# Filler products on TensorE between the stages of a two-block model

## The chip, the cores and the metric

The kernel runs on one core of a Trainium2 chip. The metric is the device time of one execution in microseconds (us), the median of the runs.

## The reference, cut to what matters

Two transformer blocks run one after the other on 512 tokens of width 1024, in float32. Every sublayer begins with an RMS norm and ends by adding to the residual `x`.

```python
h = rms_norm(x, g) @ w_in                      # first block: sparse attention with compressed keys, and latent attention
x = x + concat(o_nsa, o_mla) @ w_out
x = x + (silu(n(x) @ w_gate) * (n(x) @ w_up)) @ w_down
x = x + short_conv(n(x) @ od_w_in) @ od_w_out
x = x + moe_top2(n(x))                         # 8 experts, each token takes the two highest
# second block: a gated linear recurrence, attention with decay, and a chunked recurrence (RWKV) side by side
x = x + concat(lru, fox, rwkv) @ w_out
x = x + group_experts(n(x))                    # 4 groups of 4 experts
```

## The kernel before

The program is a row of some 27 stages. A stage (`stage`, L36) is a block with one instruction list for each engine; its engines meet each other by semaphores, and at its end all of them drain and meet at a barrier. So a stage ends when its last engine does, and the next begins a little over a microsecond later.

Large products are made by `split_product` (L552): each operand is a rounded high part and a low part in fp32r, and three products (L555, L556, L557) of 128 rows, 128 columns and 512 moving columns are accumulated. The high parts are made by ScalarE (ACT), the low parts by VectorE (DVE), so TensorE (PE) waits at the start of every such stage until the first weights and activations are split. Products of plain float32 operands, such as L391, L993 or L3478, stand in the trace as two records each, a transpose (L67, L122, L195) as one.

The stages that the change touches, in order of time, with the time at which TensorE first does real work in each: `split_features` for "ev_in" (plain products to 46, split products from 49.6); `norms_and_hidden`, the stage "ev_hidden" (to 147), whose end is set by DVE (L2158); `compressed_scores` (from 159.8), with transposes L2209, then a softmax on DVE and ACT, then transposes L2215 at 183.9; three `attention` stages, ending at 303, 416 and 1886, the last with a `beside` object that adds products of the recurrence; `add_projection` three times (419.9, 1010.9, 2013.4); `norm_transpose` three times (L122, ending at 477, 863 and 1626); `gated_parts` (484.5); `split_features` for "od_in" (870.4 to 1006); `norm_route` twice, which transposes the normed rows (L195, one tile of 128 tokens after another as DVE makes them) and multiplies them with a router of 8 or 20 columns (L204), 1066.7 to 1084 and 2071.7 to 2092; `plan_passes` twice (L993 to L1007), where DVE computes each token's place from counts that TensorE makes; `sorted_passes` twice (first split products at 1113 and 2117.7), which run the experts' weights past the gathered tokens; `second_inputs` (1628.9 to 1792); the chunked recurrence `rwkv` with its stage "rw_chunks" (L3478 and others, 1886.6 to 1994); and its last stage "rw_end" (L3582, L3585), where DVE ends with L3630.

`keep_awake` (L64) is there already: 24 transposes of the unit matrix at the start of each norm. It writes bank 7 of PSUM.

## Time and profile before

| what | value |
|---|---|
| median of 3 runs | 2325.05 us (2324.07 to 2329.28) |
| profiled execution, its time | 2320.53 us |
| its span | 2319.0 us |
| mean granted TensorE clock | 0.935 |
| TensorE matmul busy | 2068.7 us, 89% |
| VectorE, ScalarE, GpSimd busy | 1285.5, 994.2 and 185.8 us |

### The profile page before, as it was taken

How to read it: one execution, taken by the hardware profiler on the slowest of the kernel's cores; microseconds unless marked ns; L12 is line 12 of the kernel's file. 1: busy time of each engine (PE TensorE's matmuls, PEld its weight loads, DVE VectorE, ACT ScalarE, POOL GpSimd, SP SyncE). 2: the span in 40 equal slices, each digit the busy share in tenths (PEclk: the TensorE clock that was granted, in tenths of full speed). 3: DMA queues.
4: the chain of work that ended last, by engine and by line, in shares of the span. 5: the costliest groups of instructions: out<-in, count | busy, mean ns of one | idle time of the engine just before them, and what ended most of it. 6: DMA issues, size and time to landing. Idle time of an engine off the chain costs nothing. (4 is left out here: it accounts for less than half of the span.)

```text
span 2319.0 us, 31287 instructions
## 1 busy us (share of the span) xinstructions
PE 2068.7 (89%) x11611; PEld 1570.0 (68%) x11611; DVE 1285.5 (55%) x1814; ACT 994.2 (43%) x1308; POOL 185.8 (8%) x182
## 2 busy tenths in 40 slices
PE   7966898889999989997899999997898789686998
PEld 5743334668888877876777888786476359575776
DVE  3367746353133234444566666888367745525888
ACT  2135736342223222221566665774243643404774
POOL 0010000000000000000311010111112200002111
PEclk9978988989999999997899999999999789886999
DMA  8006101144144125002778777995320000126996
GB/s 249 6 14 237 47 10 45 37 127 123 43 122 127 37 83 194 1 37 83 256 269 282 278 270 281 370 391 216 88 73 28 12 1 1 74 84 174 399 373 258
DMA packets 220713, 336.29 MB, mean 145 GB/s; under 512 B 50413, under 2 KB 135309, under 8 KB 220606
## 3 DMA queue, kind: packets, MB, share of 16 engines
q1 hardware_dynamic: 213470, 314.53, 40.0%
q0 software_dynamic: 7136, 20.34, 2.3%
q8 instruction: 66, 1.08, 0.2%
q14 instruction: 41, 0.34, 0.0%
HBM read 306.82 MB, written 26.95 MB: 144 GB/s over the span
## 5 line engine op out<-in xcount | busy, mean ns | idle before, releaser
L1526 DVE TENSOR_TENSOR moe_pass_wL<-moe_pass_w,moe_pass_wH 128x2048 fp32r<-128x2048 f32 (+1 forms) x144 | 303.4, 2112 | 115.8 <-ACT moe_pass_wH L1450 111.3
L1450 ACT ACTIVATE moe_pass_wH<-moe_pass_w 128x2048 fp32r<-128x2048 f32 (+1 forms) x144 | 254.7, 1772 | 129.6 <-PE PS L557 97.2
L555 PE MATMUL PS<-moe_pass_wL,moe_pass_xgH 128*128 128x512 f32 (+1 forms) x384 | 148.3, 386 | 9.1 <-DVE moe_pass_xgL L1531 4.8
L1526 DVE TENSOR_TENSOR hm_pass_wL<-hm_pass_w,hm_pass_wH 128x2048 fp32r<-128x2048 f32 x60 | 135.9, 2288 | 34.8 <-ACT hm_pass_wH L1450 34.7
L555 PE MATMUL PS<-xnT_low,ffn_upH 128*128 128x512 f32 x352 | 140.3, 399 | 7.4 <-DVE xnT_low L873 7.1
L557 PE MATMUL PS<-moe_pass_wH,moe_pass_xgH 128*128 128x512 f32 (+1 forms) x384 | 143.5, 374 | 0.0
L556 PE MATMUL PS<-moe_pass_wH,moe_pass_xgL 128*128 128x512 f32 (+1 forms) x384 | 143.5, 374 | 0.0
L557 PE MATMUL PS<-ffn_xH,ffn_upH 128*128 128x512 f32 x352 | 139.9, 397 | 0.0
L556 PE MATMUL PS<-ffn_xH,ffn_up_low 128*128 128x512 f32 x352 | 138.4, 393 | 0.0
L1450 ACT ACTIVATE hm_pass_wH<-hm_pass_w 128x2048 fp32r<-128x2048 f32 x60 | 112.2, 1910 | 17.1 <-PEq L1340 6.0
L880 DVE TENSOR_TENSOR ffn_hT<-ffn_sg,PS 128x512 f32<-128x512 f32 x22 | 15.1, 688 | 167.7 <-PE PS L557 167.7
L839 ACT ACTIVATE ffn_sg<-PS 128x512 f32<-128x512 f32 x22 | 13.2, 599 | 187.8 <-PE PS L557 187.8
L555 PEld LDWEIGHTS PS<-moe_pass_wL,moe_pass_xgH 128*128 128x128 f32 x384 | 72.5, 189 | 28.5 <-issue 11.8
L555 PE MATMUL PS<-xnT_low,od_in_wH 128*128 128x512 f32 x192 | 77.3, 403 | 7.1 <-DVE od_W_low L689 7.1
L555 PEld LDWEIGHTS PS<-xnT_low,ffn_upH 128*128 128x128 f32 x352 | 66.6, 189 | 22.4 <-DVE ffn_up_low L858 7.3
L557 PEld LDWEIGHTS PS<-moe_pass_wH,moe_pass_xgH 128*128 128x128 f32 x384 | 72.6, 189 | 10.6
L556 PEld LDWEIGHTS PS<-moe_pass_wH,moe_pass_xgL 128*128 128x128 f32 x384 | 72.7, 189 | 9.4
L557 PEld LDWEIGHTS PS<-ffn_xH,ffn_upH 128*128 128x128 f32 x352 | 66.9, 190 | 15.9
L556 PEld LDWEIGHTS PS<-ffn_xH,ffn_up_low 128*128 128x128 f32 x352 | 66.7, 190 | 15.8
L556 PE MATMUL PS<-od_xH,od_W_low 128*128 128x512 f32 x192 | 76.7, 399 | 0.0
L555 PE MATMUL PS<-hm_pass_wL,hm_pass_xgH 128*128 128x512 f32 x160 | 65.3, 408 | 12.7 <-DVE hm_pass_wL L1526 7.1
L557 PE MATMUL PS<-od_xH,od_in_wH 128*128 128x512 f32 x192 | 75.7, 394 | 0.0
(841 smaller groups left out, 4868.6 us busy)
## 6 DMA issues: line engine op xcount, KB each, us to landing
moe_pass_w<-in_moe_w_down SPq DMA_DIRECT2D x40, 1024.0 KB, 4.9
moe_pass_w<-in_moe_w_gate SPq DMA_DIRECT2D x32, 1024.0 KB, 5.2
moe_pass_w<-in_moe_w_up SPq DMA_DIRECT2D x32, 1024.0 KB, 7.2
hm_pass_w<-in_exp_w_gate SPq DMA_DIRECT2D x40, 512.0 KB, 7.7
hm_pass_w<-in_exp_w_up SPq DMA_DIRECT2D x40, 512.0 KB, 6.9
hm_pass_w<-in_exp_w_down SPq DMA_DIRECT2D x40, 512.0 KB
od_W<-in_od_w_in SPq DMA_DIRECT2D x12, 1024.0 KB, 8.2
moe_pass_w<-in_moe_w_gate SPq DMA_DIRECT2D x16, 768.0 KB
```

Source lines behind the costliest of these rows:

```text
L555: nc.tensor.matmul(out, lh, rl, start=start, stop=False)
L556: nc.tensor.matmul(out, ll, rh, start=False, stop=False)
L557: return nc.tensor.matmul(out, lh, rh, start=False, stop=stop)
L839: nc.scalar.activation(sg[:, c % 2], PS[:, c % 2, :], ACT.Silu).then_inc(s["silu"], 1)
L880: nc.vector.tensor_tensor(hT[:, c], sg[:, c % 2], PS[:, 2 + c % 2, :], ALU.mult).then_inc(s["hidden"], 1)
L1450: nc.scalar.activation(wH[:, i % S, 0:n], w[:, i % R, 0:n], ACT.Copy).then_inc(s["high"], 1)
L1526: nc.vector.tensor_tensor(wL[:, i % S, 0:n], w[:, i % R, 0:n], f32(wH[:, i % S, 0:n]), ALU.subtract) \
```

## The change

A helper `stay_busy` issues `n` products of the unit matrix with a matrix of ones, float32, 128 by 128 by 128, into a PSUM bank that nothing reads any more or yet. Nothing reads their result. There are 18 calls of it, which come up 33 times, since helpers run more than once, with 463 products in all, in the order of TensorE's own instructions; before some of the calls stand waits, so that the bank is free. `norm_transpose` has a new semaphore `placed`, which counts its DVE copies out of PSUM. All other engines' instructions are as before.

```diff
+def stay_busy(nc, C, n, bank=7):
+    for _ in range(n):
+        nc.tensor.matmul(C.PS[:, bank, 0:P], C.ident[:, :], C.ones[:, :], start=True, stop=True)
...
 def norm_transpose(...):
...
-                                            PS[:, 2 * t + h].rearrange("p (k c) -> p k c", k=4), g, ALU.mult)
+                                            PS[:, 2 * t + h].rearrange("p (k c) -> p k c", k=4), g, ALU.mult).then_inc(s["placed"], 1)
...
                 ins.then_inc(s["turned"], 1)
+            pe.wait_ge(s["placed"], 1)
+            stay_busy(nc, C, 12, 0)
...
 def norm_route(...):
             keep_awake(nc, C)
+            stay_busy(nc, C, 16)
             turn(0)
...
 def attention(...):
                 beside.tensor_end(pe, s)
+            pe.wait_ge(s["exped"], U)
+            stay_busy(nc, C, 16 if beside else 5, 0)
...
 def add_projection(...):
         def _(pe):
+            stay_busy(nc, C, 12)
             for k in range(KD):
...
 def split_features(...):
+            if NP:
+                pe.wait_ge(s["taken"], 8)
+            stay_busy(nc, C, 12)
             for j, (w, wL, take, ready) in enumerate(jobs):
...
+            pe.wait_ge(s["taken"], NP + len(jobs) - 2)
+            stay_busy(nc, C, 6, (NP + len(jobs) - 3) % 8)
...
 def gated_parts(...):
             pe.sem_inc(s["down_free"], DR)
+            stay_busy(nc, C, 12)
...
-def plan_passes(nc, C, name, tiles, hits, token_rows, kept, pick, weigh, exps, weights=None, token_weights=None, ring=None):
+def plan_passes(nc, C, name, tiles, hits, token_rows, kept, pick, weigh, exps, busy, weights=None, token_weights=None, ring=None):
+            stay_busy(nc, C, busy[0])
             pe.wait_ge(s["masked"], 1)
...
             ins.then_inc(s["placed"], 1)
+            stay_busy(nc, C, busy[1])
             pe.wait_ge(s["hot"], 1)
...
             ins.then_inc(s["found"], 1)
+            stay_busy(nc, C, busy[2])
             if weights is not None:
...
 def sorted_passes(...):
+            stay_busy(nc, C, 8)
             n = passes(pe)
             gather(0, OVER > 0)
+            stay_busy(nc, C, 14)
...
             one_pass(n, False, True)
+            stay_busy(nc, C, 8, 3)
             pe.wait_ge(s["spots"], 1)
...
 def norms_and_hidden(...):
                 hidden(n)
+            pe.wait_ge(s["gelu"], 1)
+            stay_busy(nc, C, 40, 4)
...
 def compressed_scores(...):
                 ins.then_inc(s["by_token"], 1)
+            stay_busy(nc, C, 36, 0)
             pe.wait_ge(s["values_taken"], 2)
             pe.wait_ge(s["weighed"], 1)
...
 # plan_passes: busy is (10, 20, 16) for moe_plan and (5, 4, 20) for hm_plan
 def second_inputs(...):
             ins.then_inc(s["made"], 1)
+            stay_busy(nc, C, 12)
             for j in range(NJ):
...
+            pe.wait_ge(s["normed"], 8)
+            stay_busy(nc, C, 18)
...
 # rwkv, stage rw_end, after L3585
+                stay_busy(nc, C, 44)
```

## Rows read from the trace of the kernel before

**Rows 1.** Span and mean granted clock of the core.

```profile
core 0: 2319.0 us, clock 0.935
```

**Rows 2.** Timeline: start us, us, engine line operation, tiles, shapes, records, [idle before].

```profile
1088.06 0.64 PE L993 MATMUL PS<-moe_plan_mask,ones 128*128 128x32 f32 x2 [4.02 <-DVE moe_plan_mask L1019]
...
1095.48 0.80 PE L1001 MATMUL PS<-moe_plan_token,moe_plan_hot 128*128 128x1 f32 x3 [5.12 <-DVE moe_plan_hot L1071]
```

**Rows 3.** Window of L3478: us, PE busy (records), PEld busy, clock, DMA share, GB/s.

```profile
1909.66:1910.55 0.89, 0.89 (x8) 0.86 (x8) 1.00 0.00 0
```

**Rows 4.** Windows: us, busy (count) of PE, PEld, DVE, ACT, POOL, clock, DMA, GB/s.

```profile
469.10:472.51 3.41, 3.41 (x18) 3.41 (x17) 2.35 (x6) 2.59 (x6) 0.00 (x0) 0.50 0.66 191
472.51:475.92 3.41, 3.41 (x29) 3.13 (x28) 1.58 (x3) 3.41 (x4) 0.00 (x0) 1.00 1.16 290
```

**Rows 5.** Windows: first split products of six stages; columns as in rows 4.

```profile
49.55:52.67 3.12, 3.12 (x7) 2.48 (x8) 3.12 (x6) 0.00 (x0) 0.00 (x0) 0.50 1.12 371
419.93:424.73 4.80, 4.80 (x11) 3.76 (x12) 4.80 (x6) 4.80 (x8) 0.00 (x0) 0.50 0.79 300
484.47:489.58 5.11, 5.11 (x12) 4.05 (x13) 5.11 (x8) 4.17 (x5) 0.00 (x0) 0.50 0.37 119
870.43:875.29 4.86, 4.86 (x12) 3.79 (x13) 4.69 (x7) 2.76 (x5) 0.00 (x0) 0.50 1.07 354
1010.91:1015.23 4.32, 4.32 (x10) 3.48 (x11) 4.32 (x6) 4.32 (x7) 0.00 (x0) 0.50 0.85 337
2013.37:2018.75 5.38, 5.38 (x13) 4.23 (x14) 5.38 (x7) 5.38 (x9) 0.00 (x0) 0.50 0.00 0
sum 27.59, PE 27.59 PEld 21.78 DVE 27.42 ACT 21.43 POOL 0.00; mean PE 4.60 PEld 3.63 DVE 4.57 ACT 3.57 POOL 0.00
```

**Rows 6.** Windows: other stretches at low clock, and dense split products at 560.

```profile
159.84:165.31 5.47, 5.46 (x10) 2.89 (x11) 1.83 (x4) 0.00 (x0) 0.07 (x1) 0.50 0.00 1
183.88:185.79 1.91, 1.91 (x8) 1.54 (x8) 0.00 (x0) 0.00 (x0) 0.00 (x0) 0.50 0.00 0
335.98:359.87 23.89, 23.40 (x27) 7.83 (x25) 15.37 (x22) 2.35 (x5) 0.00 (x0) 0.50 0.19 44
1066.74:1084.03 17.29, 17.29 (x96) 17.20 (x96) 4.92 (x5) 3.37 (x6) 0.00 (x0) 0.60 0.30 121
1112.99:1117.63 4.64, 4.64 (x11) 3.68 (x12) 2.29 (x1) 1.24 (x1) 3.80 (x3) 0.50 0.99 238
1629.63:1633.05 3.42, 3.42 (x5) 1.35 (x4) 0.00 (x0) 3.42 (x7) 3.36 (x3) 0.50 0.42 138
1796.89:1800.30 3.41, 3.41 (x9) 0.94 (x8) 0.50 (x4) 1.02 (x3) 0.00 (x0) 0.50 0.61 195
1886.64:1902.70 16.06, 16.06 (x90) 11.72 (x91) 8.47 (x13) 4.23 (x13) 0.00 (x0) 0.50 0.01 2
2071.74:2092.10 20.36, 20.35 (x96) 20.23 (x96) 4.91 (x5) 3.37 (x6) 0.00 (x0) 0.50 0.48 168
560.00:640.00 80.00, 79.70 (x348) 64.89 (x347) 21.33 (x29) 17.73 (x27) 0.00 (x0) 1.00 0.18 56
```

**Rows 7.** Timeline: ends and starts of stages around six places.

```profile
149.13 0.57 ACT L2106 ACTIVATE ev_hid<-PS 128x64 f32<-128x64 f32 x4
...
157.89 0.63 DVE L2158 COPY ev_hid<-ev_hid 128x128 f32<-128x128 f32 x4
...
302.59 0.69 DVE L523 COPY ev_yT<-PS 128x512 f32<-128x512 f32 x1 [4.15 <-PE PS L419]
...
416.95 0.63 ACT L596 ACTIVATE ev_out_yH<-ev_yT 128x512 fp32r<-128x512 f32 x1 [6.26 <-PEq L42]
...
419.93 0.76 PE L555 MATMUL PS<-ev_front_low,ev_out_yH 128*128 128x512 f32 x1 [4.51 <-DVE ev_front_low L619]
...
1997.29 1.98 PE L3585 MATMUL PS<-rw_end_sq,ones 128*128 128x512 f32 x4 [0.59 <-ACT rw_end_sq L3593]
...
2008.24 1.28 DVE L3630 TENSOR_TENSOR s_yT<-rw_Bt,rw_gl 128x512 f32<-128x512 f32 x2
```

More of the change, by code:

```diff
@@ L67, in keep_awake @@
         nc.tensor.transpose(C.PS[:, 7, 0:P], C.ident[:, :], C.ident[:, :])
+def stay_busy(nc, C, n, bank=7):
+    for _ in range(n):
+        nc.tensor.matmul(C.PS[:, bank, 0:P], C.ident[:, :], C.ones[:, :], start=True, stop=True)
 def norm_transpose(nc, C, x, gain, xnT, xs, name, loads=None, gain_loaded=None, clear=None, ahead=None):
-    with ExitStack() as mem, stage(nc, name, "squared_a squared_v mean root rstd scaled turned") as (block, s):
+    with ExitStack() as mem, stage(nc, name, "squared_a squared_v mean root rstd scaled turned placed") as (block, s):
         ss = mem.enter_context(nc.sbuf_tensor(name + "_ss", [P, 4, NT], F32))
@@ L2615, in moe_top2 @@
             norm_route(nc, C, "moe_norm", x, xs, xnT, gx[:, :], wr, br[:, :], score, NE, loads, (loaded, 48), C.token_rows["moe_pass"], kept, constants)
-            Q = plan_passes(nc, C, "moe_plan", tiles, [one, two], C.token_rows["moe_pass"], kept, pick, weigh, exps, ring=ring)
+            Q = plan_passes(nc, C, "moe_plan", tiles, [one, two], C.token_rows["moe_pass"], kept, pick, weigh, exps, (10, 20, 16), ring=ring)
         w1, w2 = pair[:, 0], pair[:, 2]
@@ L2692, in moe_groups @@
             norm_route(nc, C, "hm_norm", x, xs, xnT, gx[:, :], wr, br[:, :], score, NG + NE, loads, (loaded, 80), C.token_rows["hm_pass"], kept, constants)
-            Q = plan_passes(nc, C, "hm_plan", tiles, [group], C.token_rows["hm_pass"], kept, pick, weigh, exps, w[:, :, :], C.token_weights)
+            Q = plan_passes(nc, C, "hm_plan", tiles, [group], C.token_rows["hm_pass"], kept, pick, weigh, exps, (5, 4, 20), w[:, :, :], C.token_weights)
         sorted_passes(nc, C, "hm_pass", x, xnT, ring, tiles, Q, NG, PG * F, PG, 0, 0, NG, None, store_tile)
```

## The prediction

> **What bounds the kernel now.** I read the span with its clock first: TensorE is granted 0.935 of its clock on average [rows 1], so (1 - 0.935) x 2 x 2319 = about 301 us pass at the low of its two levels, 1.2 GHz. That sets the most that any cure could give: were TensorE the last to be ready in all of them, 151 us. The other two questions are where these stretches lie, and in which of them TensorE is the one that is awaited; for those I went through windows and timeline.
>
> They lie in three kinds of place. First, six stages that begin with split products: PE waits some microseconds for the first splits and starts at 0.50, busy throughout, 27.59 us together [rows 5]. Second, the beginnings of stages with float32 products or transposes, and the two routers [rows 6]. Third, stretches where PE is busy without a break and yet at 0.50: 335.98 to 359.87, where most products use 8 of the 128 rows, and most of the two routers, whose products stream only 8 or 20 columns [rows 6]. The third kind says that a busy PE is not enough to hold the clock; the shape of the work counts. A filler has 128 rows, 128 loaded columns and 128 streamed ones, like the transposes of `keep_awake`, and a stretch of those began at 0.50 and was at 1.00 afterwards, with nothing but transposes on PE [rows 4]. So I expect a filler to count as work.
>
> **What one filler costs.** One call of a float32 product is two records [rows 2] (L993 is one call). At the high level eight records of 128 columns took 0.89 us [rows 3], 0.112 each, so a filler is 0.224 us. At the low level the hm router's 96 records took 20.36 us [rows 6], 0.212 each, and a filler 0.42. Groups of 12, 16, 36, 40 and 44 take 2.7, 3.6, 8.1, 9.0 and 9.9 us at the high level, 5.1, 6.8, 15.3, 17.0 and 18.7 at the low. All 463 are 104 or 196 us.
>
> **What covers them.** PE waits at these places anyway. In ev_out the stage's first ACT instruction is at 416.95 and the first product at 419.93 [rows 7]: 3.0 us for 12 fillers of 2.7. The four other stages that open with 12 just before split products, and ev_in behind its plain products, are built in the same way (ACT rounds, DVE subtracts, then PE). In rw_end PE is done at 1999.3 and DVE at 2009.5 [rows 7]: 10.2 us for 44 of 9.9. Before L1001 PE idles 5.12 us [rows 2]: 20 of 4.5. Where the cover fits, an edit costs nothing so long as the clock is high when the group begins; at the low level the same group is late by the whole difference.
>
> **What it takes away, step by step.**
>
> 1. First products of six stages. 65 records in 27.59 us at 0.50 [rows 5], against 80 us / 348 = 0.230 each in dense stretches [rows 6]: 27.6 - 65 x 0.230 = -12.6 us. DVE's low parts come at one per 0.64 us (8 in 5.11, the third row) and a k-step of three products takes 0.69, so PE stays the last.
> 2. Four short float32 stretches [rows 6]. The first products of the compressed scores, 5.47 us, behind 40 fillers; the last transposes there, 1.91, behind 36; the first products of second_inputs, 3.42, behind 12 of the norm; the first of the decayed attention, 3.41, behind 18. All dense, so half: -7.1 us.
> 3. The chunk stage, 1886.64 to 1902.70, 16.06 us with PE busy throughout. The 16 fillers at the end of the attention stage leave a gap of about 1 us. Half would be 8.0, but DVE is busy 8.47 us of these [rows 6] and becomes the bound in its first third: -6.0.
> 4. The routers. hm: 20.36 us at 0.50 for 96 records [rows 6]. All at the high level they would take 96 x 0.112 = 10.8, or -9.5; but its L204 products are those that let the clock fall even while PE is busy, so I keep the last third at the low level: -6.8. moe: 17.29 us at mean 0.60 [rows 6], whose middle was already at 1.00: -2.0.
> 5. Plans and passes. The counts and the one-hot products of moe_plan, and the first 4.64 us of products of its passes [rows 6], would win 2.8 + 2.1; but the plan is entered at the low level that the router leaves, and its first 10 fillers then take 4.2 us against 4.02 idle, of which only some 2.8 lie in the stage [rows 2]: +1.3. Net -3.6. In hm's I count -0.5: its passes' first products are followed by waits for weights anyway.
>
> **What it adds.** Fillers that stand at the end of a stage and are not covered. The 40 of ev_hidden wait for L2106, which ends at 149.7; DVE ends the stage at 158.5 [rows 7]. The engine had idled before, so the clock falls by then in most executions, and I let a third of the 40 run low: 149.7 + 9.0 + 2.4 = 161.1, or +2.4 (bounds: +0.2 all high, +8.2 all low). The 5 behind the first attention take 1.1 us while DVE's last copy, 0.69 us, ends the stage [rows 7]: +0.4, and again in the latent one. The other endings (6 fillers of ev_in and od_in, 12 of s_norm, 18 of second_inputs, 16 of the decayed attention) overshoot by +0.5, +0.3, +0.9, +0.5 and +0.2 by the same reckoning, which are estimates from the same kinds of rows, and the start of ev_in by +0.2. Sum: +5.8 us. The new `placed` increments ride on instructions that are there; their wait was met long before by the first copy.
>
> **The sum.** -12.6 - 7.1 - 6.0 - 8.8 - 3.6 - 0.5 + 5.8 = -32.8 us against the profiled execution's 2320.5, or 2287.7. Its own time lies 4.5 us under the median of the runs, so the same difference from the median is 2292.3. Every term supposes that the clock was high when a group began, and where in a group it changes is chance, so some of 33 places will not come off; I take off a tenth of the gain and forecast 2295 us.
>
> The Trainium skill bears on this in "TensorE: Matmul & The Clock Gate", Part 1. It says that the gate opens with activity and closes after idleness, and that for a model the ramp penalty is below 1% of a typical kernel span. By that, less than 23 us are to be had and the time is above 2302. This trace shows 27.59 us at the low level in the first kind of place alone [rows 5], and 301 in all, because every stage boundary may bring a new ramp. The trace outweighs it, and the sum above doesn't use it.
>
> **The rivals.**
>
> *Half of it* (2303 to 2315, about 2309). The idle stretches that matter are broken by a barrier of over a microsecond, in which no filler can run, and the fillers in front of and behind it may be too short in some places. Against it: with the groups in place little more than that barrier is left of the idle 4.51 us before ev_out's first product [rows 7]. If only the first kind and the short stretches come off and the costs stay, -12.6 - 7.1 + 5.8 = -13.9 us: 2311. The skill's below 1% would end in or just above this case. Chance 0.17.
>
> *The fillers run at the low level* (slower). Mechanism: each group begins after idleness, at 0.50, and the unit matrix, mostly zeros, doesn't raise it. Price: 44 fillers in rw_end take 18.7 against 10.2 of cover, the 40 in ev_hidden 17.0 against 8.8, 12 in ev_out 5.1 against 3.0: of 19.4 us that these 96 gain in length 18.8 are exposed. For all 463 that makes about 90 us and no gain: 2415. Mixed, with share p of the fillers low, gain and loss meet at 33(1 - p) = 90p, p = 0.27: from a quarter of the groups upwards the change loses. For it: most groups do begin after a wait, and the routers were at 0.50 while busy. Against it: the transposes of the same matrix raised the clock [rows 4]. Chance 0.06, and mostly near the point of balance, 2330 to 2345.
>
> *It shifts the waits only* (within 0.2%, 2320 to 2330). PE's first products come sooner, and the next wait, for weights or DVE, takes the gain back. For it: DVE is busy for nearly the whole of the six starts [rows 5]. Against it: later in such stages PE is without gaps (79.70 of 80 us from 560 on [rows 6]), so a start that is earlier by 2 us ends the stage earlier by 2 us. Chance 0.07.
>
> *All of it and more* (2275 to 2283). ev_hidden's 40 all high, hm router wholly high, moe_plan not late: -2.2 - 2.7 - 1.3 more, and no tenth lost. Chance 0.05.
>
> The forecast's own case, 2283 to 2303, has 0.65.
>
> **Range and chances.** From 2281 to 2313 it holds the main case, most of the half case and some of the last: 0.8. Faster by over 0.2% (4.65 us, about what a measurement can tell from no change) is main, half and more: 0.87. Same 0.07, slower 0.06.
>
> **What would show it right or wrong.** The mean clock should rise from 0.935 to about 0.965. The six starts should be at 1.00 with records 0.23 us apart; one at 0.50 refutes step 1 for that stage. The chunk stage should last about 6 us less until the first common record after 1902.7. In the routers the first transposes should be at 1.00, and part of L204 still at 0.50. Fillers should be 0.224 us apart; groups at 0.42 are the slow rival. After the last filler of ev_hidden and of both attentions no other engine should be the last of its stage. Wrong would be the sum, rather than the mechanism, if the clock is up and the span isn't down.

## The result and the profile after

The changed kernel takes 2293.74 us, the median of 4 executions (2289.0 to 2299.9), beside 2324.56 for the kernel before (4, 2321.4 to 2329.3). The ratio is 0.9877, with a 95% interval of 0.9849 to 0.9906: faster by 1.2%. The forecast was 2295.0, with 2281 to 2313 around it.

The first row to read is that of the core, against [rows 1]:

```profile
core 0: 2291.6 us, clock 0.970
```

The span fell by 27.4 us. Time at the low level fell from about 301 us to (1 - 0.970) x 2 x 2291.6 = about 137, so 164 us less. Two records at the high level take as long as one at the low, so work that TensorE alone holds up would have given half of that, 82 us; the span gave 27. In most of the stretches TensorE was not the engine that was waited for, or fillers were what ran in them.

The windows that begin at each of the six first split products, cut behind the same number of records as in [rows 5] (the counts in brackets are those of all records that touch the window):

```profile
48.17:49.90 1.73, 1.73 (x7) 1.42 (x8) 1.73 (x4) 0.00 (x0) 0.00 (x0) 1.00 1.05 372
411.45:414.06 2.61, 2.60 (x12) 2.15 (x12) 2.61 (x4) 2.61 (x5) 0.00 (x0) 1.00 1.01 405
473.83:476.68 2.85, 2.85 (x13) 2.33 (x13) 2.85 (x6) 2.85 (x4) 0.00 (x0) 1.00 0.65 212
857.31:860.18 2.87, 2.87 (x12) 2.36 (x13) 2.87 (x5) 2.78 (x5) 0.00 (x0) 1.00 1.08 365
995.91:998.32 2.41, 2.40 (x10) 1.96 (x11) 2.41 (x4) 2.41 (x5) 0.00 (x0) 1.00 1.02 420
1985.43:1988.54 3.11, 3.11 (x14) 2.52 (x15) 3.11 (x4) 3.11 (x6) 0.00 (x0) 1.00 0.00 0
sum 15.58, PE 15.57 PEld 12.75 DVE 15.58 ACT 13.76 POOL 0.00; mean PE 2.59 PEld 2.12 DVE 2.60 ACT 2.29 POOL 0.00
```

All six stand at 1.00 and PE is still busy throughout: nothing new is waited for, the same work is simply done at nearly twice the rate. The kernel before over the same records, in the same way up to the start of the next one, has this sum, and in its chunk stage, over the first 90 records, this row:

```profile
sum 28.16, PE 28.16 PEld 22.16 DVE 27.75 ACT 21.66 POOL 0.00; mean PE 4.69 PEld 3.69 DVE 4.62 ACT 3.61 POOL 0.00
...
1886.64:1902.81 16.17, 16.17 (x90) 11.83 (x92) 8.47 (x13) 4.34 (x13) 0.00 (x0) 0.50 0.01 2
```

Windows of the changed kernel: the chunk stage, the hm router's fillers, the router itself, and the last stretch of hm_plan:

```profile
1863.18:1873.02 9.84, 9.43 (x91) 6.96 (x93) 8.13 (x13) 4.29 (x13) 0.00 (x0) 1.00 0.00 1
2035.13:2038.90 3.77, 3.74 (x34) 3.55 (x32) 0.27 (x2) 0.21 (x1) 0.00 (x0) 1.00 0.45 56
2041.40:2061.55 20.15, 19.84 (x96) 19.51 (x96) 5.16 (x6) 3.37 (x6) 0.00 (x0) 0.52 0.47 165
2070.26:2076.30 6.04, 6.04 (x29) 6.04 (x30) 4.36 (x28) 0.42 (x2) 1.08 (x1) 0.50 0.30 88
```

The first 90 records of the chunk stage went from 16.17 us at 0.50 to 9.84 at 1.00, and the mark of a new bound is there: PE is no longer busy throughout (9.43), and DVE is busy for 8.13. The 16 fillers ahead of the hm router ran at 1.00; PE then idled 2.5 us for DVE, and the router ran its 96 records in 20.15 us, as slowly as in [rows 6]. hm_plan's last 20 fillers then ran at 0.50 for their first 6 us too, ahead of the product that spreads the weights.

Stage lengths, from the time at which the last engine ends one stage to that at which it ends the next, POOL's gathers counted (us, good to some 0.3). "Again" is a second profile of the changed kernel, below; it differs from "after" by chance alone. Stages that moved by less than 0.3 us are left out.

| stage | before | after | again |
|---|---|---|---|
| ev_in | 91.7 | 89.3 | 89.3 |
| ev_hidden | 45.5 | 46.4 | 50.7 |
| ev_compressed | 28.6 | 25.0 | 25.0 |
| first attention | 116.2 | 115.1 | 116.1 |
| latent heads | 56.7 | 53.7 | 57.1 |
| latent attention | 56.2 | 56.7 | 55.3 |
| ev_out | 51.2 | 49.0 | 49.0 |
| ffn | 372.8 | 370.4 | 370.5 |
| od_in | 140.9 | 139.0 | 140.4 |
| od_out | 51.6 | 49.7 | 49.7 |
| moe_norm | 25.6 | 23.3 | 25.3 |
| moe_plan | 19.3 | 20.0 | 19.0 |
| moe_pass | 512.2 | 509.6 | 509.7 |
| s_norm | 12.3 | 13.5 | 13.3 |
| s_in | 167.1 | 166.0 | 166.0 |
| s_fox | 90.4 | 87.9 | 89.1 |
| chunk stage | 108.3 | 103.9 | 105.3 |
| s_out | 52.1 | 49.6 | 49.6 |
| hm_norm | 30.8 | 30.3 | 21.8 |
| hm_plan | 15.9 | 17.3 | 17.1 |
| hm_pass | 207.8 | 209.9 | 209.1 |

The losses that repeat are those of hm_plan, hm_pass, s_norm and ev_hidden. In moe_plan it depends on which engine ends the stage. Before, that is POOL, with the second of two gathers:

```profile
1102.63 0.89 POOL L987 DMA_INDIRECT moe_plan_xto<-moe_pass_tokens,moe_plan_idxo  x1 [0.30 <-issue]
```

Its timeline after, on PE and POOL:

```profile
1066.11 4.03 PE L73 MATMUL PS<-ones,ident 128*128 128x128 f32 x20 [1.31 <-PEq L42]
1069.97 0.31 PE L1012 MATMUL PS<-moe_plan_mask,ones 128*128 128x32 f32 x2
...
1079.53 5.47 PE L73 MATMUL PS<-ones,ident 128*128 128x128 f32 x32
...
1082.23 0.88 POOL L1005 DMA_INDIRECT moe_plan_xto<-moe_pass_tokens,moe_plan_idxo  x1 [0.30 <-issue]
```

The last 16 fillers (32 records, L73) run from 1079.53 to 1085.00, the first 3.4 us of it at the low level, while POOL's last gather ends at 1083.11. TensorE, with filling only, ends the stage, 1.9 us late. POOL alone would have ended it 18.1 us after the stage before it, where it took 19.3 in the kernel before: the earlier groups had gained 1.2 us, and the last one spent 1.9. (The expectations below count moe_plan and moe_pass as 17.1 and 514.3 us in the kernel before; that leaves POOL's gathers out, which hold the stage open. The loss of 2.8 us in moe_plan and a part of the gain of 4.7 in moe_pass come from there.)

### The profile page after: what moved, and what is told of

It reads as the page before. It is cut to its first block and busy times, and to the rows that moved or that the text cites. A ratio compares the mean times of both kernels' runs of the same rounds, so it can differ in the third digit from the quotient of the medians.

```text
span 2291.6 us, 33139 instructions
## 1 busy us (share of the span) xinstructions
PE 2137.0 (93%) x12537; PEld 1652.5 (72%) x12537; DVE 1284.4 (56%) x1814; ACT 994.1 (43%) x1308; POOL 186.9 (8%) x182
## 5 line engine op out<-in xcount | busy, mean ns | idle before, releaser
L73 PE MATMUL PS<-ones,ident 128*128 128x128 f32 x926 | 120.9, 293 | 13.4 <-PEq L42 11.1
L73 PEld LDWEIGHTS PS<-ones,ident 128*128 128x128 f32 x926 | 116.9, 207 | 18.3 <-issue 15.4
L857 ACT ACTIVATE ffn_sg<-PS 128x512 f32<-128x512 f32 x22 | 13.2, 598 | 185.0 <-PE PS L568 185.0
L566 PE MATMUL PS<-hm_pass_wL,hm_pass_xgH 128*128 128x512 f32 x160 | 64.9, 405 | 12.6 <-DVE hm_pass_wL L1550 10.4
```

What stands on the lines that cost most here:

```text
L73: nc.tensor.matmul(C.PS[:, bank, 0:P], C.ident[:, :], C.ones[:, :], start=True, stop=True)
L566: nc.tensor.matmul(out, lh, rl, start=start, stop=False)
L857: nc.scalar.activation(sg[:, c % 2], PS[:, c % 2, :], ACT.Silu).then_inc(s["silu"], 1)
```

## The experiments

Each run is compared with executions of the kernel before on its own chip; medians of the kernel before in these comparisons lie between 2322.0 and 2324.6 us.

| run | median us | ratio, 95% | clock |
|---|---|---|---|
| narrow | 2359.9 | 1.0156 (1.0130 to 1.0182) | 0.931 |
| rows32 | 2359.1 | 1.0154 (1.0131 to 1.0177) | 0.931 |
| recur | 2316.7 | 0.9976 (0.9963 to 0.9988) | 0.940 |
| padonly | 2310.6 | 0.9947 (0.9928 to 0.9966) | 0.940 |
| nostarts | 2304.0 | 0.9918 (0.9899 to 0.9937) | 0.961 |
| starts | 2301.0 | 0.9905 (0.9880 to 0.9930) | 0.943 |
| again | 2294.8 | 0.9874 (0.9850 to 0.9897) | 0.969 |
| pad | 2291.1 | 0.9852 (0.9834 to 0.9871) | 0.971 |
| noplans | 2289.3 | 0.9856 (0.9829 to 0.9883) | 0.963 |
| planend | 2286.8 | 0.9842 (0.9827 to 0.9857) | 0.971 |
| router | 2286.2 | 0.9840 (0.9814 to 0.9866) | 0.975 |
| best | 2279.7 | 0.9830 (0.9806 to 0.9853) | 0.978 |

**Fillers of 8 columns.** All 463 fillers at their places, each with next to nothing to stream; the 128 by 128 unit matrix is still loaded for each.

```diff
-        nc.tensor.matmul(C.PS[:, bank, 0:P], C.ident[:, :], C.ones[:, :], start=True, stop=True)
+        nc.tensor.matmul(C.PS[:, bank, 0:8], C.ident[:, :], C.ones[:, 0:8], start=True, stop=True)
```

> Every filler keeps its place and its count but multiplies only 8 columns of the ones, not 128, so TensorE is given as many instructions at the same times and very little work in them. My theory, that the gain is the clock, which stays high when fillers give TensorE real work where it would idle: the granted clock goes back to that of before (0.935, against 0.970), the six split-product starts are at 0.50 again, and the time is that of before within some 6 us, 2318 to 2331 us. Rival: it is enough that TensorE is not idle, whatever it does: then the clock is 0.970 and the time about 2290 to 2294, the fillers being shorter. Rival: the gain comes from the waits and the order that the edits bring: 2294 too, but with the clock of before.

**Fillers of 32 rows.**

```diff
-        nc.tensor.matmul(C.PS[:, bank, 0:P], C.ident[:, :], C.ones[:, :], start=True, stop=True)
+        nc.tensor.matmul(C.PS[:, bank, 0:P], C.ident[0:32, :], C.ones[0:32, :], start=True, stop=True)
```

> Every filler keeps place, count and its 128 columns, but contracts over 32 rows of the unit matrix and of the ones in place of 128. It should last as long (0.27 us at the high rate). If the clock asks only whether TensorE streams columns, time and clock are those of the changed kernel, 2294 us and 0.970. If the rows in use count too, as the 12 spreading products over 8 rows suggest, behind which the clock fell while TensorE was busy without a gap, the fillers are worth a quarter: clock near 0.94 and 2320 to 2345 us, between the narrow fillers (2359.9) and the kernel before.

Both came out alike, 35 us *slower* than the kernel before. The groups of the filler line, minimum, median and maximum of a record in ns, in the changed kernel, then in the narrow one, then with 32 rows:

```profile
L73 PE MATMUL PS<-ones,ident x926: 270/275/582, 44.9 to 2281.5; 128*128 128x128 f32 x186
```

```profile
L73 PE MATMUL PS<-ones,ident x926: 170/361/381, 44.9 to 2347.1; 128*128 128x8 f32 x186
```

```profile
L73 PE MATMUL PS<-ones,ident x926: 270/416/577, 44.9 to 2355.9; 32*128 32x128 f32 x186
```

The minimum is that of the high level, the median shows where most of them ran: 275 of 270 in the changed kernel, but 361 and 416 in these two, more than half of them at the low level. (One record follows another after 0.112 us at the high level [rows 3], so records of 270 ns overlap.) By the clock's own stretches in the three traces, 99 of the 926 filler records begin at the low level in the changed kernel, 519 in the narrow one and 497 with 32 rows. The six starts took 25.55 us in the narrow kernel and 26.73 with 32 rows, against 28.16 before and 15.58 with real fillers:

```profile
sum 25.55, PE 25.55 PEld 20.16 DVE 24.88 ACT 18.02 POOL 0.00; mean PE 4.26 PEld 3.36 DVE 4.15 ACT 3.00 POOL 0.00
```

```profile
sum 26.73, PE 26.73 PEld 21.04 DVE 25.92 ACT 17.60 POOL 0.00; mean PE 4.45 PEld 3.51 DVE 4.32 ACT 2.93 POOL 0.00
```

So the order of the work, the added waits and TensorE being given instructions bring nothing. What pays is that a filler uses the array: its streamed columns and its rows both count, 8 columns are too few and so are 32 rows; nothing between these and 128 was tried. Both rivals of the narrow run fell (that it is enough not to be idle, and that the waits and the order bring the gain), and so did my size for the two: I had the narrow one back at the time of before and the one of 32 rows between, and had forgotten that a filler that does not raise the clock is itself a long one. ev_hidden went from 45.5 to 53.3 and 53.6 us, moe_plan from 19.3 to 27.4 and 28.3, the last recurrence step from 15.7 to 19.7 and 19.9. These two runs show what the prediction's slow rival costs.

**Fillers at the six starts only, and all but those.** The first keeps the groups of 12 in `norm_transpose`, `add_projection`, `split_features` and `gated_parts` and takes all others out; the second takes just these out.

```diff
-            stay_busy(nc, C, 12)        # add_projection, split_features, gated_parts
-            stay_busy(nc, C, 12, 0)     # norm_transpose
```

> Only the fillers at the split-product starts are kept (12 at the end of norm_transpose, 12 at the start of add_projection, 12 in split_features behind the pair products, 12 in gated_parts); all others are taken out. In the changed kernel the six starts together are 13.2 us shorter than in the kernel before and s_norm is 1.2 longer. If each place pays for itself alone, this version is about 12 to 14 us below the kernel before, 2310 to 2313 us, and the other fillers hold the remaining 18. Rival: places depend on one another (an earlier stage's fillers decide whether the clock is high when the next one begins): then this one is either within 5 us of the changed kernel or less than 8 below the kernel before.

> The changed kernel without the fillers at the split-product starts, the complement of the run that had only those (2301.0 us, 23.6 below the kernel before, where its own six stages were 11 to 13 us shorter in its profile). If what that run gained is these fillers' own, taking them away from the changed kernel costs as much, about 2316 us. If each place is worth only what the profiles show, 13 us, it is about 2307 us, and the remainder of that run's gain was the scatter between executions (2299.1 to 2307.8).

In the first the six windows sum to 15.93 us, five at 1.00 and one at 0.88, in the second to 25.27, five of those six at clocks of 0.51 to 0.63 and one at 0.50. The windows' rows of the two sums:

```profile
sum 15.93, PE 15.93 PEld 13.01 DVE 15.93 ACT 14.06 POOL 0.00; mean PE 2.65 PEld 2.17 DVE 2.65 ACT 2.34 POOL 0.00
```

```profile
sum 25.27, PE 25.26 PEld 19.94 DVE 25.27 ACT 20.12 POOL 0.00; mean PE 4.21 PEld 3.32 DVE 4.21 ACT 3.35 POOL 0.00
```

The starts are high because of the groups just ahead of them, and low without them. In profiled executions the two spans are 13.0 and 16.0 us under the kernel before, together 29.0, where the whole change has 27.4: the parts add up. In medians they don't: the starts alone gained 23.6 us, more than the 12 to 14 forecast and than either rival, yet taking them away cost only 10 (2304.0, where 2307 or 2316 was expected). The profiled execution of the starts alone was 6.8 us above its own median and that of the kernel before some 5 below its own. The starts are worth between 10 and 24 us by the times, 12.6 by the windows; I trust the windows.

**The recurrence alone.** 12 fillers within s_in and 18 at its end, just ahead of s_fox, and 44 in the last recurrence step, all others taken out. (The expectation puts the first two into s_fox; they stand in `second_inputs`. The 16 at the end of s_fox, which the prediction's step 3 rests on, are not in this run.)

> Only the fillers of the recurrence: 12 and 18 in s_fox and 44 in the last recurrence step; nothing else is added to the kernel before. In the changed kernel s_fox is 2.4 us shorter and the chunk stage 4.4, the last step unchanged. If these come from their own fillers the time is about 7 us below the kernel before, 2317 to 2319 us (my prediction had 6.0 less 0.2 for this part). Rival: s_fox gains from the fillers ahead of it (end of s_in), then 4 to 5 us. Rival: the chunk stage's gain comes from the stage before it: none, 2324.

The time is 6.4 us below (12 executions), and in its profile s_fox took 87.8 us and the chunk stage 103.7, as in the changed kernel (87.9 and 103.9). For s_fox the fillers just ahead of it explain that: in this run its start is at the high level, and in the profiles without them it isn't. For the chunk stage they do not. No filler runs between 1793.4 and 1990.2, and the stage still began at 0.50, but only for 6.5 us, where the kernel before had 17.2. So this run does not show where the chunk stage's gain comes from. What does is the set of profiles: the eight with the 16 real fillers ahead all began the stage at 1.00 and took 101.6 to 105.3 us; without them it was 108.3, 108.3 and 107.4, and 103.7 here, and with the fillers of 8 columns and of 32 rows 108.4 and 109.4.

**Without the fillers of plans and passes.** `stay_busy` taken out of `plan_passes` and `sorted_passes`.

> The changed kernel without the fillers of plan_passes and sorted_passes. Stage by stage from before to after, moe_plan grew by 2.8 us, moe_pass fell by 4.7, hm_plan grew by 1.4 and hm_pass by 2.0: together +1.5. If these differences are the fillers' own doing, taking them out gives 1.5 us back, about 2292 us, with moe_plan near 17.1, moe_pass near 514, hm_plan near 15.9 and hm_pass near 208. Rival: the pass differences come from where the clock happens to be high at the start of a pass and not from the fillers: then the plans fall by 4 us and the passes stay, about 2289 to 2290. Rival: fillers of the plan do hold the clock for the first pass: 2297 or more.

2289.3 us (2285.0 to 2298.3), so no slower than the changed kernel, whose 8 executions here have a median of 2294.1 (2288.6 to 2299.9). That is less than the scatter can settle, but it has *less* clock (0.963 against 0.970). By stages: moe_plan 19.2 (from 20.0 and 19.0 in the two profiles of the changed kernel), hm_plan 15.8 (from 17.3 and 17.1), moe_pass 510.9 (from 509.6 and 509.7). The pass loses 1.3 us without its groups, and the plans lose some 1 to 2 with theirs. hm_pass is 211.8, and it is 211.8 in the run of the recurrence alone too, so the 2.0 us that it had grown by are not the fillers'; the changed kernel itself also came out at 209.1.

**Fillers within the routers.**

```diff
             keep_awake(nc, C)
-            stay_busy(nc, C, 16)
+            stay_busy(nc, C, 16 if n < 16 else 28)
             turn(0)
             for t in range(1, NT):
                 turn(t)
                 logits(t - 1)
+                stay_busy(nc, C, 3)
```

> Three fillers behind each of the first three groups of logits in norm_route, in both routers, and 28 fillers instead of 16 ahead of the first turn in the second router, where TensorE idled 2.53 us behind the fillers and the clock then stayed at 0.50 through the whole router. If the low clock there comes from the little work that logits of 8 or 20 columns give TensorE, together with that idle stretch, hm_norm falls by 5 to 7 us and hm_plan by 1 to 2 (its fillers run at the high rate), moe_norm and moe_plan by 0 to 3: 2284 to 2288 us in all. Rival: the router is paced by the placing copies of ScalarE and VectorE or by loads: the added 18 fillers, at 0.22 to 0.42 us for one, lengthen it by 2 to 5 us: 2296 to 2299.

2286.2 us, within the 2284 to 2288 forecast, hm_norm 23.8 us, at 1.00 in the router. That seems to bear the expectation out. But noplans, without this edit, had 22.7, and even the run with starts only had 24.0; that is what the next run was for.

**The changed kernel again.**

> The changed kernel, word for word, for a second profile and more executions. In its first profile hm_norm took 30.3 us with TensorE at 0.50 throughout the router, but the run without fillers in the plans, with the same router, had 22.7, and the run with fillers at the starts only, with none in the router, had 24.0. If the phase of the clock is chance from one execution to the next, hm_norm can come out anywhere from 22 to 31 us here, the stages that are always at the high level repeat within 0.1 us, and the median is 2291 to 2296. If instead 30.3 us belongs to this kernel's timing, it comes out at 30 to 31 us again.

hm_norm took 21.8 us. The router's window in this profile, to be held against the third of the four rows above (20.15 us at 0.52):

```profile
2053.11:2064.82 11.71, 11.37 (x96) 10.91 (x96) 5.16 (x6) 3.36 (x6) 0.00 (x0) 1.00 0.82 286
```

The same 96 records, the same code: 11.7 us or 20.2. What differed is the wait ahead of the first transpose, here and in the first profile:

```profile
2053.11 2.35 PE L203 MATMUL PS<-ident,hm_xs 128*128 128x128 f32 x16 [0.75 <-DVE hm_xs L187]
```

```profile
2041.40 3.17 PE L203 MATMUL PS<-ident,hm_xs 128*128 128x128 f32 x16 [2.53 <-DVE hm_xs L187]
```

Here the transposes of `keep_awake` ran at the low level, took 4.48 us in place of 2.81, and so covered most of the wait. In the other profiles with 16 fillers the transposes also ran high behind a wait of 1.13 us (noplans) and with hardly any (nostarts), and low behind one of 2.25 (pad); in nostarts and noplans the clock fell later, within the router. And ev_hidden, whose 40 fillers were the largest cost in the prediction, came out at 50.7 here, 46.4 in the first profile. So a single profile cannot say what a group of fillers is worth in such a stage. Of the five profiles taken with 16 fillers ahead of this router, with or without the plan's, hm_norm had 30.3, 21.8, 22.7, 25.7 and 27.1 us. The three with the edit above had 23.8, 23.8 and 23.8. The edit costs 2 us against the best case, and in these three profiles no bad one came up.

**Router fillers, without the last group of each plan.**

```diff
-... exps, (10, 20, 16), ring=ring)
+... exps, (10, 20, 0), ring=ring)
-... exps, (5, 4, 20), w[:, :, :], C.token_weights)
+... exps, (5, 4, 0), w[:, :, :], C.token_weights)
```

> The kernel of the run with fillers in the routers, less the last group of fillers in each plan (16 behind the last products of moe_plan, 20 in hm_plan ahead of the product that spreads the weights). In the changed kernel those groups ran at the low rate, held the stage open behind POOL's gathers (moe_plan) and delayed the spreading product (hm_plan). Theory: they only cost, so moe_plan falls from 19.0 to about 16.5 us and hm_plan from 17.3 to about 15.9, the passes stay where they are, and the time is about 2282 us (2286.2 with them). Rival: they hold the clock for the start of the pass, which loses 3 to 4 us without them: 2286 again.

No gain: 2286.8 against 2286.2 us. moe_plan stayed where it was (19.3 us, from 19.0), since POOL ends it:

```profile
1085.66 0.88 POOL L1006 DMA_INDIRECT moe_plan_xto<-moe_pass_tokens,moe_plan_idxo  x1 [0.30 <-issue]
```

In the router run its last fillers had ended only 0.3 us behind these gathers, so there was next to nothing to win. hm_plan hardly moved (17.3 to 17.1), so its last 20 fillers are not what it had lost by; the first 5 are. They run at the low level and hold up the counts that DVE waits for, as these two lines of the kernel before and of the changed one show, 2.3 and 3.4 us behind the end of the stage before:

```profile
2094.71 0.61 PE L993 MATMUL PS<-hm_plan_mask,ones 128*128 128x16 f32 x2 [2.62 <-DVE hm_plan_mask L1021]
```

```profile
2064.86 0.45 PE L1012 MATMUL PS<-hm_plan_mask,ones 128*128 128x16 f32 x2
```

moe_pass went from 510.2 to 509.3 and od_in happened to be 1.3 longer. So the time is the rival's, but not for its reason: the passes lost nothing, and the theory failed in that the groups cost next to nothing where they stood.

**Padding the products of 8 rows.** The clock of the changed kernel falls at 332.1 us in the latent heads, where PE has no gap. The cure there is not a filler but rows: the same products with zeros below the 8 rows in use.

```diff
-        pick, spread = sb("pick", [P, 6, NH]), sb("spread", [NH, 6, P])
+        pick, spread = sb("pick", [P, 6, NH]), sb("spread", [P, 6, P])
...
+                             (spread[NH:P].rearrange("p a n -> p (a n)"), zero[NH:P, 0:6 * P])):
...
-        rs, tt, ec = sb("rs", [NH, 2, SEQ]), sb("tt", [NH, 2, SEQ]), sb("ec", [P, 1])
+        rs, tt, ec = sb("rs", [P, 2, SEQ]), sb("tt", [NH, 2, SEQ]), sb("ec", [P, 1])
...
+            step(nc.gpsimd.memset(rs[:, :, :], 0.0))
```

> The changed kernel, with the 12 spreading products of the latent heads contracted over 128 rows instead of 8: the two operands are padded with zeros below the 8 rows in use, which costs one memset on POOL and one small transfer, and no time on TensorE (a product of 512 columns takes 0.50 us at the high rate with either). In the changed kernel the clock falls to 0.50 at 332.1 us, with TensorE busy without a gap since 324.7 on products of 8 rows, and stays there for 17 us. If the few rows are what lets it fall, it stays at 1.00 here even though the added rows hold zeros, and the stage falls from 53.7 to 46 to 49 us, the time to 2287 to 2290 us (VectorE is busy 7.5 of 7.9 us there and takes part of the gain). Rival: zeros draw nothing and the clock falls as before: 2294. Rival: VectorE paces the stage whatever the clock: clock 1.00, stage above 52 us, 2293.

> The kernel before, without any filler, with the spreading products of the latent heads padded with zeros from 8 to 128 rows. With the fillers this made the stage 5.1 us shorter (53.7 to 48.6) and the next 2.0 longer. If the rows alone keep the clock, it holds without fillers too: the stage falls from 56.7 to 49 to 51 us and the time to 2317 to 2320 us (2323 before). Rival: without fillers the clock is low at the stage's start and the gain is under 2 us.

Timeline of PE in the changed kernel:

```profile
327.47 6.06 PE L2365 MATMUL PS<-lh_rs,ev_spread 8*128 8x512 f32 x12
333.46 2.07 PE L2362 MATMUL PS<-ev_ukv,ev_latent 128*128 128x512 f32 x2
335.46 10.61 PE L2365 MATMUL PS<-lh_rs,ev_spread 8*128 8x512 f32 x12
346.00 4.41 PE L2362 MATMUL PS<-ev_ukv,ev_latent 128*128 128x512 f32 x6
```

and of the padded one:

```profile
329.46 5.42 PE L2367 MATMUL PS<-lh_rs,ev_spread 128*128 128x512 f32 x12
334.71 1.02 PE L2364 MATMUL PS<-ev_ukv,ev_latent 128*128 128x512 f32 x2
335.57 5.31 PE L2367 MATMUL PS<-lh_rs,ev_spread 128*128 128x512 f32 x12
340.72 2.74 PE L2364 MATMUL PS<-ev_ukv,ev_latent 128*128 128x512 f32 x6
...
348.74 5.04 PE L400 MATMUL PS<-ev_km,xnT 96*128 96x128 f32 x10 [5.28 <-PEq L42]
```

The windows of the two, before and behind the place where the clock fell in the changed kernel:

```profile
324.71:332.11 7.40, 7.40 (x18) 2.50 (x17) 3.85 (x6) 2.59 (x3) 0.00 (x0) 1.00 0.09 22
332.11:349.18 17.07, 17.07 (x20) 5.83 (x19) 13.47 (x19) 1.20 (x2) 0.00 (x0) 0.50 0.22 52
```

```profile
329.46:343.50 14.04, 14.00 (x33) 5.99 (x32) 12.27 (x18) 4.38 (x7) 0.00 (x0) 1.00 0.20 47
347.63:354.46 6.83, 5.72 (x13) 3.82 (x14) 3.59 (x13) 2.39 (x9) 0.00 (x0) 0.50 0.70 245
```

In the changed kernel PE is busy for 17.07 of 17.07 us and stands at 0.50. Padded, the second group of 12 records takes 5.31 us where it took 10.61, and the stage 48.6 where it took 53.7. The rows that were added hold zeros, and they count all the same. In the eleven profiles without padding this stage took 53.7 to 57.1 us, in the three with it 48.5, 48.5 and 48.6. The last two rows of the padded kernel (L400 in its timeline, 347.63 in its windows) show a part of the gain given back: PE now idles 5.28 us, mostly because the transfers and DVE's products into `ev_km` are still on their way (to 347.5 and 347.9), and the attention starts at the low level (58.6 us against 56.7). The median is 3 us under the changed kernel's, too little to tell from its scatter; the stage shows the gain.

In the kernel without fillers padding made the stage 48.5 us, from 56.7, and the next 54.9, from 56.2; the ratio is 0.9947. I had expected a median 3 to 6 us lower, and it is 11.4 lower. The two stages' 8.2 and 1.3 us are seen in the profile; the remaining 2 us are within the interval (8 to 17 us) and need no cause.

**Put together.** The edits of router, planend and pad, and in the latent heads, where TensorE has nothing to do behind its last product:

```diff
             value(3)
+            pe.wait_ge(s["k_roped"], 2)
+            stay_busy(nc, C, 20, 0)
```

> Put together: the changed kernel, with fillers in both routers, no last group of fillers in the plans, the padded spreading products, and 20 fillers at the end of the latent heads, where TensorE waits 5.3 us for the transfers into the keys and the clock then fell for 6.8 us at the start of the attention. The run with routers and shorter plans stood at 2286.8; padding took 2.7 us off the changed kernel's median (5.1 off its stage, 2.0 of it given back in the next); the new group should keep those 2.0. Sum: 2286.8 less 5 is about 2281 to 2283 us. Rival: the parts share their gain, 2286 us.

2279.7 us, 14 under the changed kernel and 42 under the one before:

```profile
core 0: 2277.9 us, clock 0.978
```

The latent attention is back at 56.7 us from 58.6, the 2 us that were expected of the new group, moe_plan is at 18.8 and hm_norm at 23.8. The forecast of 2281 to 2283 lay a little above the measured median.

## Why the prediction was right

The change was to keep the clock up by real work for the array, and that is what it did. The sum was -32.8 us less a tenth, or -29.5 against the median; measured were -30.8 between medians and -27.4 between the two profiled executions. Step by step:

1. *First products of six stages, -12.6.* 28.16 to 15.58 us: -12.6, and the six stages are 13.2 shorter in one profile and 11.7 in the other. The case for reading the rate of dense stretches into the cold ones ([rows 5], [rows 6]) holds.
2. *Four short float32 stretches, -7.1.* ev_compressed -3.6, as costed (3.7): 25.0 us in all eight profiles with the 36 and 40 fillers, 28.2 to 28.6 in the four without any there. s_in -1.1, which s_norm's +1.2 takes back: its first products were at the high level in both profiles, but s_in was also 164.4, 165.5 and 166.1 us in the three other kernels without the fillers of the norm (nostarts, padonly, recur), so this gain is not shown to be the fillers'. s_fox -2.4 and -1.3. Together some -7 and -6, before s_norm's cost.
3. *The chunk stage, -6.0.* -6.3 over the first 90 records, as DVE becomes the bound; the stage fell by only 4.4, because a short stretch at 0.50 came back some 50 us later, from 1915.9 on, and by 3.0 in the second profile. The recurrence alone had 4.6 without the fillers of this step, by a low stretch that happened to be short.
4. *The routers, -8.8.* The size of this term was wrong in both profiles, in both directions: hm_norm -0.5 and -9.0 for -6.8, moe_norm -2.3 and -0.3 for -2.0. (Two thirds of 9.5 are also 6.3 and not 6.8.) The step said "the last third at the low level". What the runs show is that the whole router can be at one level or at the other: low behind 2.53 us of idleness between the 16 fillers and the first transpose, high behind 0.75. That the wait decides it is likely but not shown. Over five profiles hm_norm lay between 21.8 and 30.3 us.
5. *Plans and passes, -4.1.* Right for moe, wrong for hm. moe_plan was to win 1.5 net; up to POOL's last gather it had won 1.2 in the first profile, and the last group, which was not costed, ended the stage 1.9 us behind that: +0.7, and -0.3 in the second profile. moe_pass was to win 2.1 and won 2.6 and 2.5; without its fillers 1.3. hm was to win 0.5: hm_plan lost 1.4 and 1.2, since its first 5 fillers delay the counts by 1.1 us, which was not costed, and hm_pass grew by 2.1 and 1.3 with or without fillers. In all +1.6 and -0.3.
6. *What it adds, +5.8.* ev_hidden +0.9 and +5.2 around the +2.4 predicted (its own terms add up to 2.6), within its bounds of 0.2 and 8.2. Three other kernels without fillers there (padonly, recur, starts) had 46.6, 46.7 and 47.1 us, though, so in the first profile they may have cost nothing. s_norm +1.2 for 0.9. The first attention lost nothing, the latent one +0.5 and -0.9 for the 0.4 predicted.

The 3.0 us that the latent heads gained in the first profile were no part of the sum, and in the second they were not there (57.1 us): chance, for the eleven profiles of these same instructions lie between 53.7 and 57.1. The missing gains of the hm router and of the plans and passes (6.3 and 5.7 us in the first profile) were partly made up by such stages and by the tenth taken off. That the total came within 1.3 us of the forecast is in good part luck.

Of the rivals, *half of it*, which kept only the starts and the short stretches, is refuted by the chunk stage and by moe_pass. *It shifts the waits only* is refuted where it was to show: PE has no new gaps behind the starts. *All of it and more* was priced from the profiled execution: 6.2 us under 2292.3 would be 2286, not 2275 to 2283. *The fillers run at the low level* is what narrow and rows32 come to; with real fillers it did not happen (99 of 926 records), and the argument that decided it, that a stretch of `keep_awake`'s transposes had begun at 0.50 and left at 1.00 [rows 4], was the right one. These two runs put its price lower: 90 us were forecast with all 463 at the low level, and 35 were measured with a little over half of the records there; rw_end lost 4.0 and 4.2 where 8.5 was costed, and the six starts were 2.6 and 1.4 us shorter even so.

The Trainium skill, in "TensorE: Matmul & The Clock Gate", Part 1, has the ramp penalty below 1% of a typical kernel span. Here the fillers alone took off 1.2%, and the last version 1.7%, with 100 us still at the low level. This kernel has some 27 stages, and in the trace before the clock is low at the beginning of many of them ([rows 5], [rows 6]), so the trace and not the rule of thumb was the thing to go by. The page also puts its advice as one on gaps in PE's work. In the row of 332.11:349.18 PE has no gap and stands at 0.50, and the run with 32 rows gives TensorE the same instructions at the same places as the changed kernel and loses all that they brought. "No gaps" is not enough.

## What to carry to other kernels

Before adding fillers, read the granted clock by stretches and ask of each stretch at the low level whether TensorE is the one that is awaited there; fillers pay just ahead of dense work, inside a wait that is longer than they are at the *low* level, and as the last thing in a stage only where another engine ends later. When you ask which engine ends a stage, count the gathers of GpSimd too. Give fillers all rows and columns; those of 8 columns and of 32 rows were worse than none. Where narrow products are themselves what lets the clock fall, pad them with zero rows before thinking of fillers. And take more than one profile: one stage here differed by 8.5 us between two executions of the same code, and a stage table from one profile will hand that to whatever edit is being tried.

## What the runs showed of the hardware

Three things that I had not expected. Zeros count: products over 128 rows of which 120 hold zeros kept the clock at 1.00 where the same products over 8 rows let it fall, in the kernel with and in the one without fillers, and took no longer (0.45 us for one of 512 columns, 5.42 / 12). The unit matrix was already a hint of this. A quarter of the rows is worth as little as a sixteenth of the columns: fillers over 32 rows with 128 columns and those over 128 rows with 8 columns gave 2359.1 and 2359.9 us and the same clock, 0.931, below that of the kernel without any (0.935). And a higher mean clock is not a shorter time: noplans has 0.963 and 2289.3 us, the changed kernel 0.970 and 2294.1. The times may be equal within the scatter, but the 0.7 points of clock did not buy any.
